# Second layer's attention: scores of a step pair together, four passes for maxima among them, then both value pieces

## The reference, cut to what matters

```python
def one_block(args):
    qn, qr = args
    s = (jnp.einsum('bqhd,bkhd->bhqk', qn, k_nope)
         + jnp.einsum('bqhr,bkr->bhqk', qr, k_rope)).astype(jnp.float32) * scale
    p = jax.nn.softmax(s, axis=-1).astype(v.dtype)
    return jnp.einsum('bhqk,bkhd->bqhd', p, v)
```

## Time and profile before

| | |
|---|---|
| median of 3 runs | 4322.28 us (4321.28 to 4325.61) |
| profiled execution, its span | 4323.5 us |
| mean granted TensorE clock | 0.956 |
| TensorE busy | 3949.5 us, 91% |
| DVE busy | 2669.1 us, 62% |
| ACT busy | 2122.4 us, 49% |
| POOL busy | 1204.6 us, 28% |
| second attention, first to last score or value matmul | about 3000 to 4045 us |

### The profile page before, as it was taken

The page is one execution under the profiler, slowest core; times in us unless marked ns, Lnnn a source line. Parts: engine busy times, 40 slices in busy tenths (PEclk is TensorE's granted clock), DMA queues, the critical chain, the costliest instruction groups (busy, mean ns, idle before and its releaser), DMA issues. The chain is left out here.

```text
span 4323.5 us, 76198 instructions
## 1 busy us (share of the span) xinstructions
PE 3949.5 (91%) x31096; PEld 2780.8 (64%) x31096; DVE 2669.1 (62%) x5092; ACT 2122.4 (49%) x3127; POOL 1204.6 (28%) x966
## 2 busy tenths in 40 slices
PE   7989999878988998888789899898999999999889
PEld 5767776546666666666477687686555555555567
DVE  5555555556777787788675323345677777777543
ACT  4444444397777888787443322222333333333431
POOL 1111111125344344434111000000444445454200
PEclk9999999887999999999789999999999999999999
DMA  3334233402111111211255544465232323231243
GB/s 124 95 115 131 83 99 102 124 20 50 34 42 39 47 44 37 56 44 48 86 181 186 197 138 147 167 217 175 52 77 54 80 61 77 55 81 34 99 141 107
DMA packets 388093, 404.95 MB, mean 94 GB/s; under 512 B 115776, under 2 KB 287488, under 8 KB 387488
## 3 DMA queue, kind: packets, MB, share of 16 engines
q1 hardware_dynamic: 386656, 396.77, 31.3%
q10 hardware_dynamic: 1088, 3.32, 0.2%
HBM read 248.36 MB, written 151.62 MB: 93 GB/s over the span
## 5 line engine op out<-in xcount | busy, mean ns | idle before, releaser
L142 ACT ACTIVATE PT<-psum 128x1024 f32<-128x1024 f32 x384 | 394.3, 1027 | 659.6 <-PE psum L132 659.1
L170 DVE TENSOR_REDUCE m<-psum 128x1 f32<-128x1024 f32 x384 | 467.9, 1221 | 274.8 <-PE psum L132 274.8
L132 PE MATMUL psum<-xc,wah 128*128 128x512 f32 x1600 | 514.8, 403 | 3.2 <-DVE xc L146 2.9
L146 POOL TENSOR_TENSOR part<-PT 128x1024 f32<-128x1024 f32 x144 | 341.5, 2371 | 471.4 <-DVE all L146 379.1
L132 PE MATMUL psum<-PT,V 128*64 128x512 f32 x1536 | 371.5, 605 | 0.0
L143 ACT ACTIVATE bias<-score,cand,cols 128x2048 bf16<-128x2048 f32 (+6 forms) x217 | 314.8, 1451 | 85.9 <-DVE cand L153 79.5
L146 POOL TENSOR_TENSOR Lm<-gm,cst 64x512 f32<-64x512 f32 x192 | 257.6, 1342 | 349.9 <-PE psum L132 194.2
L132 PEld LDWEIGHTS psum<-xc,wah 128*128 128x128 f32 x1600 | 300.0, 190 | 79.4 <-issue 10.3
L143 ACT ACTIVATE sgn<-score,cand,cols 128x1920 bf16<-128x1920 f32 (+6 forms) x217 | 291.4, 1343 | 89.5 <-DVE cand L153 84.8
L132 PE MATMUL psum<-hc,w4h 128*128 128x512 f32 x1024 | 320.3, 394 | 8.7 <-DVE w4l L146 8.7
L132 PE MATMUL psum<-xc,wal 128*128 128x512 f32 x800 | 315.9, 395 | 0.0
(11 more groups left out here) (336 smaller groups left out, 8664.9 us busy)
## 6 DMA issues: line engine op xcount, KB each, us to landing
raw_a<-in_w_a SPq DMA_DIRECT2D x50, 512.0 KB
raw_w<-in_w_in SPq DMA_DIRECT2D x32, 512.0 KB, 5.3
QNh<-scr_qnh SPq DMA_DIRECT2D x48, 256.0 KB, 4.9
QRh<-scr_qrh SPq DMA_DIRECT2D x96, 128.0 KB, 4.6
QNl<-scr_qnl SPq DMA_DIRECT2D x48, 256.0 KB, 6.4
xin<-in_x SPq DMA_DIRECT2D x16, 512.0 KB
scr_AR<-AR SPq DMA_DIRECT2D x32, 256.0 KB, 2.2
scr_BK<-BK SPq DMA_DIRECT2D x32, 256.0 KB, 2.2
```

Source lines behind the costliest of these rows:

```text
L132: return self.e.matmul(out, a, b, start=start, stop=stop, skip_group_check=True)
L142: return self.e.activation(out, src, f, bias=bias, scale=scale)
L146: return self.e.tensor_tensor(out, a, b, op) if self.e else self.vector(out)
L170: return self.e.tensor_reduce(out, a, AX, op, negate=negate) if self.e else self.vector(a)
```

## The change

The list is built pair by pair. Both steps' scores follow each other; four passes for maxima lie among them, at places given by `with_s[(g, e, at)]`: before the first matmul of the first step's half 0, before the third part (`x = 2`) of its half 1, before the rotary part of the second step's half 0, and behind its half 1. Then come `sum` or `rc` where the unit has them (two `rc` in each of pairs 2 and 3), both value pieces of the pair before, `acc` of steps `2p - 1` and `2p`, then `fold` and `half` in pair 0, `out` in pair 3. What is computed and the number of instructions stay as they were.

```diff
--- before.py
+++ after.py
@@ -2757,34 +2757,35 @@
         with_s = {}
         order_5 = [("gat", 0), ("load", 1)] + with_row(passes[:16])
         passes = passes[16:]
-        for g in range(NST + 8):
-            u, r = divmod(g, 8)
-            if g < NST:
+        for p in range(NST // 2 + 1):
+            u, r = divmod(p, 4)
+            if p < NST // 2:
                 if r == 0 and u + 2 < NUN:
                     order_5.append(("load", u + 2))
                 if r == 0 and u:
                     order_5.append(("gat", u))
-                order_5.append(("s", g))
-            many = 3 if g < 4 else 2
-            now, passes = passes[:many], passes[many:]
-            if now:
-                with_s[g] = now[0][1:]
-            order_5 += with_row(now[:many - 1])
-            if 1 < g < NST + 2:
-                order_5.append(("pv", g // 2 - 1, g % 2))
+                for g in (2 * p, 2 * p + 1):
+                    order_5.append(("s", g))
+                    now, passes = passes[:2], passes[2:]
+                    for at, k in zip(((0, 0), (1, 2)) if g % 2 == 0 else ((0, 3), (1, 5)), now):
+                        with_s[(g,) + at] = k[1:]
+                    order_5 += with_row(now)
+                    if g < 4:
+                        order_5 += with_row(passes[:1])
+                        passes = passes[1:]
+            if u and r == 1:
+                order_5.append(("sum", u - 1))
+            if u and r > 1:
+                order_5 += [("rc", u - 1, 2 * r - 4), ("rc", u - 1, 2 * r - 3)]
+            if p:
+                order_5 += [("pv", p - 1, 0), ("pv", p - 1, 1), ("acc", 2 * p - 1)]
+            if p < NST // 2:
+                order_5.append(("acc", 2 * p))
+            if u and r == 0:
+                order_5 += [("fold", u - 1), ("half", u - 1, 0), ("half", u - 1, 1)]
             if u and r == 3:
-                order_5.append(("sum", u - 1))
-            if u and r > 3:
-                order_5.append(("rc", u - 1, r - 4))
-            if u and r == 7:
                 order_5.append(("out", u - 1))
-            order_5 += with_row(now[many - 1:])
-            if 1 < g < NST + 2:
-                if r == 1:
-                    order_5.append(("fold", u - 1))
-                order_5.append(("acc", g - 2))
-            if u and r == 2:
-                order_5 += [("half", u - 1, 0), ("half", u - 1, 1)]
+        order_5 += [("sum", NUN - 1)] + [("rc", NUN - 1, x) for x in range(4)] + [("out", NUN - 1)]
         seq_max = [k[1:] for k in order_5 if k[0] == "max"]
         num_max = {k: n for n, k in enumerate(seq_max)}
         NM = 2 * NT
@@ -2822,7 +2823,7 @@
 
 
         mix2 = Mix("m2", "y2T", A["w_out2"], scratch["x1"], A["final_g2"], False)
-        done = order_5.index(("acc", NST - 1)) + 1
+        done = order_5.index(("fold", NUN - 1)) + 1
         end_5 = order_5[done:]
         assert [k[0] for k in end_5] == ["half"] * 2 + ["sum"] + ["rc"] * 4 + ["out"]
         order_5 = order_5[:done] + order_m[:1] + end_5[:3] + order_m[1:3] + end_5[3:]
@@ -2918,6 +2919,12 @@
                 t = q.mm(bank[max_at(n) + a], QRh[s % 3][ps, qs], KS[ps, 512 * x:512 * x + 512], False, True)
             t.then_inc(*q_pe.up("max", v, b, x))
 
+        def max_in_s(q, g, e, at):
+
+            if (g, e, at) in with_s:
+                max_nope(q, *with_s[(g, e, at)])
+                max_rope(q, *with_s[(g, e, at)])
+
         def pe_5(q):
             for k in order_5:
                 what = k[0]
@@ -2935,12 +2942,11 @@
                         q.wait_ge(q_act, "exp", g - 1, e)
                         ks = slice(512 * e + 128 * j, 512 * e + 128 * j + 128)
                         for x, (K, Q) in enumerate(((KNh, QNh), (KNl, QNh), (KNh, QNl))):
+                            max_in_s(q, g, e, x)
                             for a in range(2):
                                 ps = slice(64 * a, 64 * a + 64)
                                 q.mm(bank[2 * e + a], K[h % 2][ps, ks], Q[u % 3][ps, qs], x == 0, False)
-                        if e and g in with_s:
-                            max_nope(q, *with_s[g])
-                            max_rope(q, *with_s[g])
+                        max_in_s(q, g, e, 3)
                         q.wait_ge(d_qrh[u % 3], u, 3)
                         q.wait_ge(d_qrl[u % 3], u, 1)
                         q.wait_ge(d_mrow[v % 4], v, 1)
@@ -2949,6 +2955,7 @@
                                 ps = slice(64 * a, 64 * a + 64)
                                 t = q.mm(bank[2 * e + a], K[ps, ks], Q[u % 3][ps, qs], False, K is KE)
                         t.then_inc(*q_pe.up("s", g, e))
+                        max_in_s(q, g, e, 5)
                 elif what == "max" and k[1:] not in with_s.values():
                     max_nope(q, *k[1:])
                     max_rope(q, *k[1:])
```

## The result

| | before | after |
|---|---|---|
| median | 4322.23 us | 4451.98 us (4444.78 to 4465.16) |
| ratio, 95% interval | | 1.0298 (1.0284 to 1.0311) |
| profiled execution, its span | 4323.5 us | 4449.6 us |
| mean granted TensorE clock | 0.956 | 0.942 |

The changed kernel is 130 us slower. The forecast was 46 slower, the range ended at 4424. The direction was right and the size was not: 84 us are missing, and the rest of this document is about where they come from.

A forecast was written before the change was run, and what follows sets the result against it. TensorE's matmul stream was taken as the stage's bound. Regrouping (-1.20), third-pass waits (+0.76) and late DVE chores (+0.99, +1.41, +0.27) gave +2.23 us per unit, +46 in total: 4368 us, 8-in-10 range 4318 to 4424.

The forecast's parts named there:

- The bound and the stream: TensorE's stream bounds the stage; each change of kind there and back costs 0.30 us, regrouping saves 1.20 per unit.
- The turnaround of a pass: Maxima passes share one PSUM buffer: turnaround 2.05 us, so each pair's third pass waits 0.19, 0.76 per unit.
- The chores behind the fourth reduction: DVE chores delay the next pair's TensorE: lost 0.99 us behind pair 2, 1.41 pair 3, 0.27 pair 0.
- the threshold: DVE's room for chores behind a pair's fourth reduction: 3.16 us before the next first reduction is late.
- Their sum: Regrouping, pass waits and late chores: -1.20 + 0.76 + 0.99 + 1.41 + 0.27 = +2.23 us per unit, +46 in total.
- POOL gets in: Pair 3: POOL's addition takes the SBUF side before `out`, which waits 2.38 us; 50 more, 4418; chance 10%.
- a single case in another stage: POOL operation asked at 596.24, ended 598.41, behind a DVE operation started later; cited against POOL getting in.
- The clock: TensorE's 1.4 us gaps lower its clock; one 28-slot pair per unit at 1.2 GHz adds 5.5 us; 4484; chance 3%.
- SP, ACT and the data: SP's writes and loads were costed at nothing; exponentials don't bind, scores free after 1.50 us, next use 1.86 us away.

The follow-up runs named there:

- e7: Against e6: each maxima reduction reads 768 of 1024 columns, exponential scale a twentieth, so another attention is computed; 4281.99 us, ratio 0.9902.
- e1: Against the changed kernel: `out` moved ahead of both `acc` in pair 3, behind the two `rc`; 4374.33 us, ratio 1.0119.
- e6: Against the changed kernel: `rc` spread, `out` ahead of both `acc`, `fold` behind the first reduction of pair 1; 4310.83 us, ratio 0.9968.
- e4: Against the changed kernel: the four `rc` spread behind first and third reductions of pairs 2 and 3, `out` still last; 4363.87 us, ratio 1.0100.
- e2: Against the changed kernel: TensorE repeats two matmuls 13 times in pair 0's gap, units 2 to 22; 4414.56 us, ratio 1.0213.
- e3: Against the changed kernel: `out` moved between the two `acc` of pair 3; 4451.61 us, ratio 1.0299.

## Why the prediction was wrong

- **The bound and the stream** (one visit instead of two, 0.30): right in kind, small in size. It is 0.44 per pair without any waits (e7), 1.76 a unit instead of 1.20.
- **The turnaround of a pass** (2.05, third pass 0.19 late): right in kind. In e1 and e6 no pass but the third waits where chores are on time, and taking a fifth off the reduction's time takes these waits away (e7). They cost 1.17 a unit (e6 against e7) and not 0.76: the first slot behind such a wait takes 0.34 instead of 0.23 as well, and the slots between waits come at 0.232 instead of 0.228.
- **The chores behind the fourth reduction**: right for pairs 0, 1 and 2, and for pair 3 where POOL stays out. From before the gap to the second slot behind it e1 loses 3330.89 - 3328.89 - 2 x 0.23 = 1.54 us behind pair 3, where the forecast has 1.41; read in the same way, it is 0.96 behind pair 2 (0.99) and 0.38 behind pair 0 (0.27). e4 shows it from the other side: below the threshold the wait is gone.
- **Their sum** agrees better than its terms. A unit was forecast at 45.52 us and is 45.55 in e1, and the kernel with just this mechanism takes 4374 where the forecast was 4368; but the regrouping gains 0.56 more than was thought, and the waits cost about 0.6 more. That these cancel is luck.
- **POOL gets in** is the step that failed. The sum has `out` at 0.61 us behind the two `acc`, on DVE alone; it took 2.85, because POOL's waiting addition went first. As a rival it was priced well (2.38 a unit; it is 2.06, or 43 us over 21 units) and given 10% on the strength of a single case in another stage (called there, it stands in the earlier trace rows; the rows of SP are the earlier trace rows). There DVE's next operation, of 1024 columns, went ahead of a POOL operation whose record had started. In this stage POOL went first in every unit of the traces, with `out` (the changed kernel, e2, e4) or with `acc` (e3) as DVE's next. The Trainium skill (SBUF — State Buffer, "SBUF: two separate sides"), which the prediction names beside this rival, says that whoever starts first has the ports for the whole instruction. e3 agrees with it if a waiting POOL counts as first; the earlier trace rows, read in that way, do not. What made the difference in the earlier trace rows was not tried and stays open.
- **The clock** was weighed as a rival on its own, against gaps of 1.4 us, and there it was rightly put low: e1 has such gaps and the clock holds. The failure is that the two rivals were treated as separate. With POOL's 2.06 the gap grows to 3.64 us, and behind it 7 to 13 slots run at 0.43. e2 priced this at 37 us; the forecast's sum has nothing for it, and the range of 8 in 10 left it out. The three together, 46 + 21 x 2.06 + 37 = 126, come within 4 us of the 130 that were measured.
- **SP, ACT and the data**: cost nothing, as forecast; no wait of TensorE for a DMA or an exponential stands among the long ones in the stage.

## What to carry to other kernels

Grouping like work on one engine groups the chores of the engine that feeds it, too: add them up against the time that is left between two of its urgent operations, and spread them, rather than look at its mean load. Where an operation of VectorE can be held up by one of GpSimd, as `out` is here, put it ahead of the operation that releases GpSimd: `out` ahead of both `acc` took 0.69 us instead of 2.85. And when one rival can set off another, price them together as well: here the gap that POOL lengthened brought the lower clock with it.

## What the hardware showed that had not been expected

- A DVE operation of four columns (`negm`, both inputs in SBUF, 0.16 us alone) takes 1.75 us when a POOL addition runs (e6). Beside such additions the reductions from PSUM keep their 1.22 (e6, 3320.36) and the reciprocals their 0.95 (e4, 3322.17), and so does `fold`, with one input in PSUM and one in SBUF, its 0.68 (e6, 3325.74).
- Adding 26 matmuls a unit made the kernel 37 us faster (e2), because they stood in a gap behind which the granted clock was 0.50 without them. Gaps of 1.65 (e1) and 2.05 us (e4) in the same place left it at 1.00. Of 42 gaps of 3.63 to 3.66 us, in the changed kernel and e3, 40 were followed by slots at 0.43 and two were not.
- A wait costs a little beyond its length: the first slot behind one takes 0.35 instead of 0.23 (3330.54 to 3330.89 in e1), and where no pass waits the slots of a pair come at 0.228 instead of 0.232 (e7).
